# A mixture-of-experts kernel: each expert block's list of places is read into the partitions in another order

## The chip, the cores and the metric

The kernel runs on one core of a Trainium2 chip. The metric is the time of one execution on the device in microseconds (us), as the median of several runs. The engines of the core are called PE (TensorE, matmuls; its weight loads are shown apart as PEld), DVE (VectorE), ACT (ScalarE), POOL (GpSimd) and SP (SyncE, which here only issues transfers). Transfers run on the core's 16 DMA engines, whoever issues them.

## What is computed

One hybrid decoder layer over 16 + 512 tokens of width 1024: a mixer of gated short convolutions and a state-space scan, then a mixture of experts, top 4 of 32, and a final norm. All of it is float32. The change touches only the mixture of experts:

```python
top_vals, top_idx = lax.top_k(logits, TOP_K)              # 4 experts for each of 512 tokens
...
def run_block(args):
    tok, g, e = args
    xb = xt[tok]
    gu = xb @ w_gate_up[e] + b_gate_up[e]
    glu = jnp.minimum(gu[:, :D_FF], SWIGLU_LIMIT)
    lin = jnp.clip(gu[:, D_FF:], -SWIGLU_LIMIT, SWIGLU_LIMIT)
    act = glu * jax.nn.sigmoid(SWIGLU_ALPHA * glu) * (lin + 1.0)
    return (act @ w_down[e] + b_down[e]) * g[:, None]
```

So each expert has 12 MB of weights (1024x2048 and 1024x1024 in float32), which are read once, and gets on average 2048 / 32 = 64 rows of the tokens.

## The kernel before

The mixer runs first (up to about 460 us), then norm, routing and the mixture of experts. What follows is about the last.

**Blocks.** The tokens of an expert take places in a block of `BLOCK` = 96 places, filled from place 0 on; an expert with more than 96 tokens would get more blocks. With these inputs no expert has more than 96, so there are 32 blocks, one for each expert. What is left of a block is unfilled: its entries in `slot_table` hold numbers beyond the range of rows, and the indirect transfers skip them.

**Lanes.** The 1024 columns of a token are cut into `LANES` = 4 quarters of 256 columns (1 KB). Quarter l lives in partitions 32 l to 32 l + 31. A partition holds `GRANULES` = 3 places of the block, 32 x 3 = 96. Which three places stand in which partition is set by how the list is read: `list_rows` reads the 96 entries (token row, output row) once for each lane into `idx_raw`, 32 partitions of 6 integers. Before, partition r of a lane (r = 0 to 31) gets places 3r, 3r + 1, 3r + 2.

**Rows in and out.** For each expert `gather` issues three indirect DMAs (granule n = 0, 1, 2), each of which reads one 1 KB row of `n2_d` (shown as `n_scratch` in the trace) into every partition whose place is filled. `scatter` issues three that write the 1 KB results back into `expert_rows`. Both go through POOL's queue. Around them POOL reads the next list (four DMAs), then waits until lists, rows and results have landed, and passes the lists on through a chain of small copies (`idx_next`, `mid2`, `mid1`, `idx_now`).

**The product.** PE computes a block as 192 products: the 96 rows of the block are the stationary side, in groups of 32 columns, the weights stream past. `TURNS` = "GGGGDDGGDDGGDDDD" weaves the 8 gate-and-up pieces (G) of block j with the 8 half pieces (D) of the down product of block j - 1. DVE turns and bounds what comes out (from L1426 on), ACT does the sigmoid (L927) and copies the down product out (L933, `evict`), which needs `y_room`, POOL's mark that the results before have left.

**The weights.** SP issues the weights as six DMAs of 2 MB for each expert (L498 and L502) into a ring of twelve 1 MB slots. Each waits (L411, `hold`) until PE has used what stood in its slots, and PE waits with `pair_here` until a pair of slots has landed, which is when all 16 DMA engines have delivered their share.

The first two experts don't gather: PE picks their tokens by a product with the 0/1 matrices `chosen` and `chosen1`, made by comparing each token's place with `slot_iota` and `slot_iota1`. Those two hold the numbers of the places in the order in which the block's columns stand, so they have to follow the order of the lists.

Of the kernel before, what the change touches and what calls it, by code (L numbers as in the profile page):

```python
# [33 lines left out]
ds = bass.ds  # L34
# [16 lines left out]
BLOCK = 96  # L51
FIRST, SECOND = 0, 1
BLOCKS_MAX = -(-SEQ // BLOCK)
CAPACITY = BLOCKS_MAX * BLOCK
# [8 lines left out]
LANES, LANE = 4, 32  # L63
GRANULES = BLOCK // LANE
QUARTER = D // LANES
FF_LANE = D // LANES
FF_BLOCKS = FF_LANE // LANE
SLOTS = 6
HALF = LEN // 2
CHALF = (SEQ + 4) // 2  # L70

# [34 lines left out]
def build(nc, xT_d, xrow_d, par_d, wdt_d, win_d, wout_d, rows_d, rw_d, rb_d, moe_d, bgu_d, bd_d, out_d):  # L106
    ctx = ExitStack()
    with ctx:
        def sem(name):
            return ctx.enter_context(nc.semaphore(name))  # L110

        def sb(name, shape, dt=F32):
            return ctx.enter_context(nc.sbuf_tensor(name, shape, dt))
# [4 lines left out]
        table_d = nc.dram_tensor("slot_table", [EXPERTS * CAPACITY + P, 2], I32).ap()  # L118
# [4 lines left out]

        with nc.sbuf_tensor("ring_r", [P, SLOTS * PIECE], F32R) as ring_r:
            pass
        ring = sb("ring", [P, SLOTS * PIECE])
        with nc.sbuf_tensor("late_r", [P, XBC_TILES * LEN], F32R) as late_r:
# [24 lines left out]
        def slot(s):  # L152
            return ring[:, s * PIECE:(s + 1) * PIECE] if s < SLOTS else ring2[:, (s - SLOTS) * PIECE:(s - SLOTS + 1) * PIECE]

        def two_slots(h):
            s = 2 * h
            return ring[:, s * PIECE:(s + 2) * PIECE] if s < SLOTS else ring2[:, (s - SLOTS) * PIECE:(s - SLOTS + 2) * PIECE]

        def one_piece(e, q):
            return moe_d[e, q // 2, :, q % 2 * PIECE:(q % 2 + 1) * PIECE]  # L160
# [3 lines left out]
        def view(region, at, *shape):  # L164
            n = int(np.prod(shape))
            v = region[:, at:at + n]
            if len(shape) == 2:
                v = v.rearrange("p (a b) -> p a b", a=shape[0])
            if len(shape) == 3:
                v = v.rearrange("p (a b c) -> p a b c", a=shape[0], b=shape[1])  # L170
            return v
# [40 lines left out]
        slot_iota = view(late_a, 8192, BLOCK)  # L212
# [3 lines left out]
        slot_iota1 = view(late_a, 8320, BLOCK)  # L216
# [47 lines left out]
        def yk(m, hf):  # L264
# [89 lines left out]
        idx_in, idx_moved, x_in, xT_ready, lane_ready = (  # L354
            sem("idx_in"), sem("idx_moved"), sem("x_in"), sem("xT_ready"), sem("lane_ready"))
# [25 lines left out]
        PART_BANK = [0, 6, 2, 4]  # L381
        HELD = [10, 10, 6, 2, 2, 2] + [0] * (PIECES - SLOTS)
        Z_AT = [(0, 0), (1, 0), (0, 1), (1, 1), (2, 0), (2, 1), (3, 0), (3, 1)]
        Z_USE = [9, 9, 5, 1]

        def pair(k, hf, n):
            return bank[:, 2 * (k % 2) + hf, 0:n]
# [10 lines left out]
        def _(sp):  # L398
# [68 lines left out]
            for m in range(TT):  # L467
                if m == TT - 1:
                    for n in range(4):
                        sp.wait_ge(wout_used, 5 + n)  # L470
                        for q in (2 + n, SLOTS + n):
                            sp.dma_start(slot(q), one_piece(0, q)).then_inc(w_in[q], 16)
# [81 lines left out]
        def _(pool):  # L554
            steps = Steps(pool, pool_steps)
            g = nc.gpsimd
# [9 lines left out]
                            pattern=[[-1, P]], channel_multiplier=1).then_inc(consts, 1)  # L566

            g.affine_select(out=mask[:, :], in_=mask[:, :], compare_op=ALU.is_ge, fill=0.0, base=0,
                            pattern=[[1, P]], channel_multiplier=-1).then_inc(consts, 1)
            g.affine_select(out=lt_bf[:, :], in_=ones_bf[:, :], compare_op=ALU.is_gt, fill=0.0, base=0,  # L570
                            pattern=[[1, P]], channel_multiplier=-1).then_inc(consts, 1)
# [31 lines left out]
            with pool.Fori(1, TT) as i:  # L603
# [1 line left out]
                g.tensor_copy(chunk, xbc[:, :, ds(i * P + META, P)]).then_inc(chunk_ready, 1)  # L605
            pool.wait_ge(chunk_ready, TT)
            pool.wait_ge(tok_done, 2)
            g.iota(slot_iota, pattern=[[1, GRANULES], [GRANULES, LANE]], base=0, channel_multiplier=0,
                   allow_small_or_imprecise_dtypes=True).then_inc(slot_iota_ready, 1)
            g.iota(slot_iota1, pattern=[[1, GRANULES], [GRANULES, LANE]], base=CAPACITY, channel_multiplier=0,  # L610
                   allow_small_or_imprecise_dtypes=True).then_inc(slot_iota_ready, 1)


# [17 lines left out]
            def list_rows(base):  # L631

                for l in range(LANES):
                    pool.dma_start(idx_raw[l * LANE:(l + 1) * LANE, :],  # L634
                                   table_d[ds(base, BLOCK), :].rearrange("(r g) t -> r (g t)", g=GRANULES)).then_inc(idx_in, 16)

            def lane_rows():
                return g.tensor_tensor(idx_next[:, :], idx_raw[:, :], lane_off[:, :], ALU.add)
# [17 lines left out]

            mid1, mid2 = idx_kept
            list_rows(2 * CAPACITY)
            pool.wait_ge(lane_ready, LANES)
            pool.wait_ge(idx_in, 16 * LANES)  # L660
            lane_rows().then_inc(idx_moved, 1)
            pool.wait_ge(idx_moved, 1)
            gather()
            move_rows(mid2, idx_next)
            list_rows(0)
            pool.wait_ge(idx_in, 2 * 16 * LANES)
            g.tensor_tensor(idx_now[:, :], idx_raw[:, :], lane_off[:, :], ALU.add).then_inc(idx_moved, 1)
            pool.wait_ge(idx_moved, 3)
            list_rows(CAPACITY)
            pool.wait_ge(idx_in, 3 * 16 * LANES)  # L670
            g.tensor_tensor(mid1[:, :], idx_raw[:, :], lane_off[:, :], ALU.add).then_inc(idx_moved, 1)
# [14 lines left out]
            with pool.Fori(0, n_blocks - 1) as j:  # L686
# [3 lines left out]
                base = pool.value_load(blocks[0:1, ds(2 * j + 8, 1)], min_val=0, max_val=EXPERTS * CAPACITY)  # L690
# [16 lines left out]
        def _(act):  # L707
# [5 lines left out]
            for c in range(0, KC, 2):  # L713
# [4 lines left out]
            act.sem_inc(free_b, 1)  # L718
            a.activation(t1.rearrange("p (h l) -> p h l", h=2), bank[:, 0:2, 0:HALF], ACT.Sqrt, scale=1.0 / D,
                         bias=eps_col[:, 0:1]).then_inc(rs_root, 1)  # L720
# [15 lines left out]
            def take_tile(i, t):  # L736
                act.wait_ge(tile_done, i * A_TILES + t + 1)
                for hf in range(2):
                    ins = a.copy(stage[:, 3 + hf * HALF:3 + (hf + 1) * HALF], pair(t, hf, HALF))
                    if hf == 0:  # L740
# [780 lines left out]
        def _(pe):  # L1521
# [5 lines left out]
            def mm3(out, n, c, first, width):  # L1527

                for m, (w, x) in enumerate(((w_hi, n_hi), (w_hi, n_lo), (w_lo, n_hi))):
                    ins = mm(out, w[:, n % 2, c * P:(c + 1) * P], x[:, c, first:first + width],  # L1530
                             start=c == 0 and m == 0, stop=c == KC - 1 and m == 2)
                return ins
# [10 lines left out]
            for c in range(KC):  # L1543
# [4 lines left out]
                for hf in range(2):  # L1548
                    ins = mm(bank[:, hf, 0:HALF], ones[:, :], sq8[:, c, hf * HALF:(hf + 1) * HALF],
                             start=c == 0, stop=c == KC - 1)  # L1550
# [4 lines left out]
            def part(t, w, x, c, first, last):  # L1555

                for hf in range(2):
                    ins = mm(pair(t, hf, HALF), w[:, t, c * P:(c + 1) * P], x[:, c, hf * HALF:(hf + 1) * HALF],
                             start=first, stop=last)
# [26 lines left out]
            def a_tile(i, t):  # L1586
                pe.wait_ge(wl_ready, i * A_TILES + t + 1)
                pe.wait_ge(free[t % 2], i * 2 + t // 2 + 1)
                for hf in range(2):
                    for c in range(KC):  # L1590
                        ins = mm3(pair(t, hf, HALF), t, c, hf * HALF, HALF)
                ins.then_inc(tile_done, 1)
# [445 lines left out]
```

## Time and profile before

| | us |
|---|---|
| median of 3 runs | 1506.52 (1505.2 to 1506.59) |
| the profiled execution | 1505.53 |
| its span, first to last instruction | 1503.8 |
| PE busy, matmuls | 1483.7 (99%) |
| of it the experts' products, L1849 | 995.5 |
| POOL busy | 336.4 (22%) |
| TensorE clock granted, mean | 0.999 |

The profiled execution lies 1.0 us under the median. "Busy" of PE is a modelled figure, since matmuls are pipelined, and doesn't tell a PE at its peak from one that is held up a little. An engine's idle time before an instruction is put down to what released it; "issue" is time in which the engine waited for nothing that the profile shows.

### The profile page before, as it was taken

Reading aid. Unit: us, or ns where it says so; the run is one execution under the profiler, and the core shown is the slowest. Engines: PE = TensorE matmul, PEld = TensorE weight load, DVE = VectorE, ACT = ScalarE, POOL = GpSimd, SP = SyncE. Lnnn points to the kernel's source line nnn. Section 1 sums busy time; section 2 is a strip of 40 time slices with the busy share of each in tenths; the row PEclk is TensorE's granted clock in tenths of the full one; section 3 lists DMA queues with packets and bytes.
Section 4 is the critical chain, followed back from the end, with each engine's and each line's share of the span. In section 5 each row is a group of like instructions: output and inputs, shape, how many; then the busy total and the mean of one; then the engine's idle time right before and its main releaser. Section 6 shows DMA issues by size and latency. Waiting matters only on the chain.

```text
span 1503.8 us, 37254 instructions
## 1 busy us (share of the span) xinstructions
PE 1483.7 (99%) x15435; PEld 1069.7 (71%) x15435; DVE 621.5 (41%) x1269; ACT 255.4 (17%) x348; POOL 336.4 (22%) x518
## 2 busy tenths in 40 slices
PE   8999999999999999999999999999999999999998
PEld 6998998977873346777777776777856566567764
DVE  6667988868445322223222232223222232222336
ACT  3533433356231000000000000000000000000002
POOL 1000000000022252223322233222322223222240
PEclk9999999999999999999999999999999999999999
DMA  3642333331438999999999999999999999999977
GB/s 137 245 159 92 113 113 112 131 121 61 164 115 317 400 418 418 416 424 418 419 421 413 425 411 419 415 425 415 422 416 416 413 425 415 416 421 416 424 280 283
DMA packets 53993, 484.31 MB, mean 322 GB/s; under 512 B 14590, under 2 KB 15234, under 8 KB 21570
## 3 DMA queue, kind: packets, MB, share of 16 engines
q1 hardware_dynamic: 38690, 459.13, 74.4%
q0 software_dynamic: 15264, 24.63, 4.4%
q8 instruction: 28, 0.46, 0.1%
q14 instruction: 11, 0.09, 0.0%
HBM read 467.54 MB, written 25.00 MB: 328 GB/s over the span
## 4 chain that ended last, share of the span: by engine, by line
PE 90%; DMA 4%; DVE 4%; issue 1%; ACT 1%; SPq 0%; DVEq 0%; ACTq 0%
PE bank L1849 64%; PE bank L1530 15%; PE bank L1721 6%; DMA n_scratch<-reg_b 1%; DMA ring<-in_moe 1%; DMA ring<-in_w_in 1%; DVE w_lo L983 1%; PE bank L1658 1%; PE bank L1661 1%; PE bank L1673 0%; PE bank L1958 0%; PE bank L1659 0%; PE bank L1688 0%; DVE reg_tq L1073 0%; DMA block_list<-more_i 0%
## 5 line engine op out<-in xcount | busy, mean ns | idle before, releaser
L1849 PE MATMUL bank<-ring,moe_f 128*32 128x512 f32 (+1 forms) x12216 | 995.5, 485 | 4.3 <-DMA ring<-in_moe 2.7
L1849 PEld LDWEIGHTS bank<-ring,moe_f 128*32 128x32 f32 x12216 | 665.6, 110 | 333.2 <-issue 191.5
L1426 DVE STREAM_TRANSPOSE moe_f<-bank 128x768 f32<-128x768 f32 x32 | 31.5, 983 | 700.9 <-PE bank L1849 693.8
L1530 PE MATMUL bank<-n_hi,w_hi 128*128 128x258 f32 (+2 forms) x608 | 190.6, 313 | 3.3 <-DVE w_lo L983 3.3
L1530 PE MATMUL bank<-n_lo,w_hi 128*128 128x258 f32 (+2 forms) x608 | 186.3, 306 | 0.0
L1530 PE MATMUL bank<-n_hi,w_lo 128*128 128x258 f32 (+2 forms) x608 | 186.3, 306 | 0.0
L927 ACT ACTIVATE moe_f<-moe_f 128x768 f32<-128x768 f32 x32 | 27.0, 845 | 830.0 <-DVE moe_f L1432 830.0
L642 POOL DMA_INDIRECT moe_f<-n_scratch,idx_next x96 | 105.7, 1101 | 267.3 <-DVE moe_f L1408 242.4
L1530 PEld LDWEIGHTS bank<-n_hi,w_hi 128*128 128x128 f32 x608 | 114.4, 188 | 11.3 <-issue 3.5
L1530 PEld LDWEIGHTS bank<-n_lo,w_hi 128*128 128x128 f32 x608 | 114.5, 188 | 6.9 <-issue 1.7
L1530 PEld LDWEIGHTS bank<-n_hi,w_lo 128*128 128x128 f32 x608 | 114.4, 188 | 5.5
L649 POOL DMA_INDIRECT expert_rows<-moe_f,idx_now x93 | 95.1, 1022 | 35.4 <-issue 31.7
L655 POOL COPY idx_now<-idx_kept 128x6 int32<-128x6 int32 x31 | 5.8, 187 | 339.3 <-DMA expert_rows<-moe_f,idx_now 339.3
L634 POOL DMA_DIRECT2D idx_raw<-slot_table x140 | 72.4, 536 | 14.1 <-DMA n_scratch<-reg_b 13.5
L619 POOL DMA_INDIRECT slot_table<-val,pos_i x16 | 16.6, 1041 | 196.9 <-DVE pos_i L1326 193.2
L983 DVE TENSOR_TENSOR w_lo<-ring,w_hi 128x1024 fp32r<-128x1024 f32 x48 | 58.4, 1218 | 5.1 <-ACT w_hi L728 5.1
L728 ACT CAST w_hi<-ring 128x1024 fp32r<-128x1024 f32 x48 | 50.4, 1053 | 54.0 <-PE bank L1530 50.5
L1436 DVE TENSOR_SCALAR moe_f<-moe_f 128x96 f32<-128x96 f32 x256 | 51.9, 302 | 0.0
L1432 DVE TENSOR_SCALAR moe_f<-moe_f 128x96 f32<-128x96 f32 x256 | 47.5, 260 | 0.0
L1445 DVE TENSOR_TENSOR moe_f<-moe_f 128x768 f32<-128x768 f32 x32 | 30.7, 958 | 32.3 <-remote 28.2
L1721 PE MATMUL bank<-ring_r 128*128 128x512 f32 x128 | 41.8, 408 | 0.0
L933 ACT COPY moe_f<-bank 128x768 f32<-128x768 f32 x31 | 24.8, 800 | 91.4 <-remote 74.6
(293 smaller groups left out, 1054.1 us busy)
## 6 DMA issues: line engine op xcount, KB each, us to landing
ring<-in_moe SPq DMA_DIRECT2D x184, 2048.0 KB
ring<-in_w_in SPq DMA_DIRECT2D x24, 1024.0 KB, 4.9
ring<-in_moe SPq DMA_DIRECT2D x13, 1024.0 KB, 8.5
expert_rows<-reg_k POOLq DMA_DIRECT2D x8, 1024.0 KB, 6.5
ring<-in_w_out SPq DMA_DIRECT2D x8, 1024.0 KB, 4.8
ring<-expert_rows SPq DMA_DIRECT2D x8, 1024.0 KB, 12.1
ring<-acs_scratch SPq DMA_DIRECT2D x4, 1024.0 KB, 7.0
idx_raw<-slot_table POOLq DMA_DIRECT2D x140, 0.8 KB
```

What stands on the lines that cost most here:

```text
L634: pool.dma_start(idx_raw[l * LANE:(l + 1) * LANE, :], table_d[ds(base, BLOCK), :].rearrange("(r g) t -> r (g t)", g=GRANULES)).then_inc(id ...
L642: g.indirect_dma_start(out=xg[:, n, :], out_offset=None, in_=n2_parts, in_offset=bass.IndirectOffsetOnAxis(ap=idx_next[:, 2 * n:2 * n + 1] ...
L649: g.indirect_dma_start(out=yk_parts, in_=y_sb[:, n, :], in_offset=None, out_offset=bass.IndirectOffsetOnAxis(ap=idx_now[:, 2 * n + 1:2 * n ...
L728: a.copy(w_hi[:, n % 2, :], slot(s)[:, t * KC * P:(t + 1) * KC * P]).then_inc(wh_ready, 1)
L983: v.tensor_tensor(w_lo[:, n % 2, :], slot(s)[:, t * KC * P:(t + 1) * KC * P], w_hi[:, n % 2, :].bitcast(F32), ALU.subtract).then_inc(wl_re ...
L1426: v.transpose(glu.rearrange("p b (g r) -> p g b r", g=GRANULES), gate).then_inc(gate_raw, 1)
L1432: ins = v.tensor_scalar(glu[:, b, :], glu[:, b, :], bias_col(0, b), LIMIT, ALU.add, ALU.min)
L1436: ins = v.tensor_scalar(up[:, b, :], up[:, b, :], bias_col(1, b), 1.0 - LIMIT, ALU.add, ALU.max)
L1445: v.tensor_tensor(act_last if last else act_t, up, sig, ALU.mult).then_inc(act_ready, 1)
L1530: ins = mm(out, w[:, n % 2, c * P:(c + 1) * P], x[:, c, first:first + width], start=c == 0 and m == 0, stop=c == KC - 1 and m == 2)
L1721: ins = mm(bank[:, 2 * m + hf, :], y, w[:, cols], start=t == 0 and n == 0, stop=t == 2 * KC - 1 and n == 2)
L1849: ins = mm(out[l * LANE:(l + 1) * LANE, g * width:(g + 1) * width], x[:, at, g * LANE:(g + 1) * LANE], w[:, l * width:(l + 1) * width], st ...
```

## The change

The list of 96 entries is read into the same 32 partitions of each lane, in the same runs of three entries, but in another order. With `PARTS` = 8, partition r = 4a + b of a lane (a = 0 to 7, b = 0 to 3) now gets places 3(8b + a) to 3(8b + a) + 2. The four partitions 4a to 4a + 3 of a lane so hold one run out of each quarter of the block, where before they held four neighbouring runs. The two `iota` patterns number the columns in the same new order.

```diff
+PARTS = 8
...
-            g.iota(slot_iota, pattern=[[1, GRANULES], [GRANULES, LANE]], base=0, channel_multiplier=0,
+            g.iota(slot_iota, pattern=[[1, GRANULES], [GRANULES, PARTS], [GRANULES * PARTS, LANE // PARTS]], base=0, channel_multiplier=0,
                    allow_small_or_imprecise_dtypes=True).then_inc(slot_iota_ready, 1)
-            g.iota(slot_iota1, pattern=[[1, GRANULES], [GRANULES, LANE]], base=CAPACITY, channel_multiplier=0,
+            g.iota(slot_iota1, pattern=[[1, GRANULES], [GRANULES, PARTS], [GRANULES * PARTS, LANE // PARTS]], base=CAPACITY, channel_multiplier=0,
                    allow_small_or_imprecise_dtypes=True).then_inc(slot_iota_ready, 1)
...
                 for l in range(LANES):
                     pool.dma_start(idx_raw[l * LANE:(l + 1) * LANE, :],
-                                   table_d[ds(base, BLOCK), :].rearrange("(r g) t -> r (g t)", g=GRANULES)).then_inc(idx_in, 16)
+                                   table_d[ds(base, BLOCK), :].rearrange("(b a g) t -> a b (g t)", a=PARTS, g=GRANULES)
+                                   ).then_inc(idx_in, 16)
```

No instruction is added, removed or moved on any engine. POOL's queue in the loop over the experts, from the gather of the next rows to the scatter, stands so before (`moe_f` is the tile of rows in and out, `slot_table` the lists, `expert_rows` the results):

```order
L642 DMA moe_f<-n_scratch,idx_next 128x256 x3
L690 ISA
L690 TENSOR_LOAD blocks
L690 ISA x2
L634 ISA
L634 DMA idx_raw<-slot_table 32x6 x4
L593 REGISTER_ALU
L649 DMA expert_rows<-moe_f,idx_now 8192x256 x3
```

And the same place in POOL's queue after the change (line numbers are one or two higher):

```order
L644 DMA moe_f<-n_scratch,idx_next 128x256 x3
L692 ISA
L692 TENSOR_LOAD blocks
L692 ISA x2
L635 ISA
L635 DMA idx_raw<-slot_table 32x1x6 x4
L594 REGISTER_ALU
L651 DMA expert_rows<-moe_f,idx_now 8192x256 x3
```

Nothing moved; only the pattern of the four list reads has a level more, with the same 6 integers (24 bytes) as its innermost run. Which partitions the three gathers and the three scatters find filled is data, and no row of this kind shows it.

## Rows read from the trace of the kernel before

**Rows 1.** The page: groups of instructions by line (count, busy us, mean ns, idle before)

```profile
L1849 PE MATMUL bank<-ring,moe_f 128*32 128x512 f32 (+1 forms) x12216 | 995.5, 485 | 4.3 <-DMA ring<-in_moe 2.7
```

**Rows 2.** Waits of SP's queue, whole span: us, times, longest us

```profile
SPq L411 <- PE bank L1849: 604.7, 134, 15.7
```

**Rows 3.** Stages: us, engines' busy us (count), clock, DMA share, GB/s

```profile
555.00:1085.00 530.00, 530.00 (x6544) 389.79 (x6540) 129.48 (x360) 27.98 (x34) 157.36 (x239) 1.00 1.01 419
1085.00:1425.00 340.00, 340.00 (x4131) 214.31 (x4127) 77.55 (x213) 17.24 (x21) 99.39 (x152) 1.00 1.00 418
```

**Rows 4.** Waits of the weight loads from 555 to 1085 us, all there are

```profile
engine line waited for: us in total, times, longest us
PEld bank L1849 <- issue: 87.9, 453, 0.6
```

**Rows 5.** Waits of the weight loads from 1085 to 1425 us, all there are

```profile
PEld bank L1849 <- issue: 61.2, 244, 0.6
PEld bank L1849 <- DMA ring<-in_moe: 5.9, 10, 0.8
```

**Rows 6.** Timeline of DVE: L1426, which follows each expert's last G piece

```profile
549.66 0.98 DVE L1426 STREAM_TRANSPOSE moe_f<-bank 128x768 f32<-128x768 f32 x1 [26.00 <-PE bank L1849]
...
580.97 0.98 DVE L1426 STREAM_TRANSPOSE moe_f<-bank 128x768 f32<-128x768 f32 x1 [23.25 <-PE bank L1849]
...
923.56 0.98 DVE L1426 STREAM_TRANSPOSE moe_f<-bank 128x768 f32<-128x768 f32 x1 [22.53 <-PE bank L1849]
...
954.52 0.98 DVE L1426 STREAM_TRANSPOSE moe_f<-bank 128x768 f32<-128x768 f32 x1 [22.76 <-PE bank L1849]
...
1078.89 0.98 DVE L1426 STREAM_TRANSPOSE moe_f<-bank 128x768 f32<-128x768 f32 x1 [22.76 <-PE bank L1849]
```

**Rows 7.** The same, the last expert of the loop

```profile
1424.70 0.98 DVE L1426 STREAM_TRANSPOSE moe_f<-bank 128x768 f32<-128x768 f32 x1 [22.54 <-PE bank L1849]
```

**Rows 8.** DMA from 1085 to 1425 us: packets, MB, share of 16 engines

```profile
DMA packets 13913, 142.01 MB, mean 418 GB/s; under 512 B 4086, under 2 KB 4138, under 8 KB 5614
...
q1 hardware_dynamic: 9337, 135.97, 95.5%
q0 software_dynamic: 4576, 6.04, 4.9%
```

**Rows 9.** Timeline of POOL over one expert

```profile
802.32 1.11 POOL L642 DMA_INDIRECT moe_f<-n_scratch,idx_next  x1 [8.03 <-DVE moe_f L1408]
...
806.25 2.07 POOL L634 DMA_DIRECT2D idx_raw<-slot_table  x4
808.62 1.05 POOL L649 DMA_INDIRECT expert_rows<-moe_f,idx_now  x1 [0.30 <-issue]
...
823.36 0.19 POOL L655 COPY idx_now<-idx_kept 128x6 int32<-128x6 int32 x1 [11.06 <-DMA expert_rows<-moe_f,idx_now]
```

**Rows 10.** Timeline of ACT: the eviction that needs POOL's mark

```profile
837.37 0.80 ACT L933 COPY moe_f<-bank 128x768 f32<-128x768 f32 x1 [2.21 <-remote]
```

**Rows 11.** Waits of the weight loads on weights at the start, 480 to 555 us

```profile
PEld bank L1849 <- DMA ring<-in_moe: 4.5, 2, 2.7
```

## The prediction

> **What bounds the kernel now.** I read the page first. The experts' products hold PE for 995.5 us and PE is said to be idle before them for 4.3 us only [rows 1], so the page alone says "PE". But SP's queue waits for PE to free ring slots in 134 cases [rows 2], while the 16 DMA engines are full: their busy share is 1.01 and 1.00 in both long stretches of the expert loop, at 419 and 418 GB/s [rows 3]. PE and the weight stream are therefore nearly matched, and the question is which of them sets the pace where. The waits of the weight loads answer that. From 555 to 1085 us they never wait for weights [rows 4]. From 1085 to 1425 us they wait for weights 10 times, 5.9 us in all, about once for each of the 11 experts [rows 5]. The marks of DVE's first transpose, one for each expert, give the pace. From 580.97 to 1078.89 there are 16 experts in 497.9 us, 31.12 us each; from 1078.89 to 1424.70 [rows 6, 7] there are 11 in 345.8 us, 31.44 us each. The shortest distance, as from 923.56 to 954.52, is 30.96 us [rows 6]: that is PE undisturbed.
>
> So the reader should see two regimes with the same mean DMA load: first PE alone sets the pace at 31.12 us, and for the last 11 experts the weights come too late, at 31.44 us. A shortage that starts only after 17 experts, with nothing else changed, is a backlog: somewhere a stream needs 31.44 us for an expert that PE asks for every 31.12 us, falls back by 0.32 us each time, and after 16 experts (5.1 us) has used up the time by which weights used to be early. The mean share can't show it, because a pair of slots counts as landed only when the slowest of the 16 engines has delivered. If the mean engine were the slow one, evening out would help nothing; if some engines carry more than the mean, it does.
>
> **What the change moves.** From the reference's inputs I worked out how many places each expert fills: 44 to 85 of 96, 2048 in all. For the eight groups of four partitions in a lane, and with two lanes together (eight partitions), the rows that an indirect gather or scatter of all three granules moves are, as a mean over the 32 experts, before: 24, 24, 24, 23.6, 19, 10, 3.4, 0.1. After: 18.5, 18.0, 17.4, 16.5, 15.3, 14.8, 14.2, 13.4. The sum is the same, 128. I assume that one DMA engine serves one such group in two lanes (32 partitions apart), so that eight of the sixteen have nearly always been full and two empty. Nothing in the rows names engines; what speaks for it is the backlog above, which needs some engines above the mean. The Trainium skill, "DMA: Bandwidth & Descriptors", The descriptor swizzle, gives this very assignment for 128-partition transfers (four neighbouring partitions and the four 32 above them go to one engine); no row here shows it for indirect ones.
>
> *Rows on the busiest engine.* POOL's queue (q0) takes 4.9% of 16 engines over 340 us [rows 8], 16.7 us per engine. At 31.44 us an expert, 340 us are 10.8 experts, so 1.54 us per engine and expert, 24.7 us over all 16. It moves 6.04 MB / 10.8 = 0.56 MB, some 546 rows of 1 KB: 45 ns a row (lists and completion marks are in this, so it is a little high; without them, nearer 40). The busiest engine had 24 in and 24 out, 48 rows, 2.2 us. After, it has 37 rows, 1.7 us. That takes 0.5 us (0.45 at 40 ns) from each expert on the busiest engine.
>
> *What the weights then allow.* The busiest engines need 31.44 us an expert now; less 0.5 that is 30.94 us, under the 31.12 us of PE's own pace, and the backlog doesn't form. Even 0.2 us would do, since the backlog of 5.1 us would then need over 40 experts. So the size of this term doesn't matter, only its sign and that it reaches the slowest engines.
>
> *Gain in the loop.* The last 11 experts go from 31.44 to 31.12 us: 3.5 us. The 5.9 us of waits [rows 5] are an upper bound, as a weight load may wait a little before PE does; PE's own figure of 2.7 us [rows 1] for such waits is a lower one. I take 3.5.
>
> *The start.* The second expert's product waits for weights twice, 4.5 us [rows 11]. That is the time for megabytes of first loads. One gather (third expert, 53 tokens) lies in front of them: on the busiest engine 24 rows become 18, 0.27 us at most. I take 0.1.
>
> *The list reads.* Four a block, 2.07 us of POOL [rows 9]. Their pattern has a level more, which no row here prices. Lower bound nothing; upper bound that each costs double, 2.1 us more of POOL before the scatter. POOL passes its waits at 823.36 us [rows 9] and the eviction that needs its mark starts at 837.37 us [rows 10], so 14 us cover it. The runs stay 24 bytes, so I take nothing. The two `iota` are single instructions well before their use: nothing. PE, DVE and ACT do the same on other columns: nothing.
>
> *More packets.* Eight filled partitions of an engine become five or six, so a packet may hold fewer rows. Lower bound nothing, upper bound one packet more per indirect DMA, six per expert, at the mean of q0, 16.7 x 16 us / 4576 = 58 ns [rows 8]: 0.35 us per expert. Even that leaves 0.15 us of the 0.5 and would merely slow the backlog: 0.17 us an expert instead of 0.32, used up after 30 experts, that is at the end. I take nothing.
>
> Sum against the profiled execution: 1505.5 - 3.5 - 0.1 = 1501.9 us. The median of the runs is 1.0 us above it, so 1502.9 us there, -0.24%.
>
> **Rivals.**
>
> *No change.* The slow stream is not a few engines but all of them: 418 to 419 GB/s in both regimes [rows 3] could be the limit of the whole path, and the busy share leaves no idle time anywhere. Or the filled partitions are dealt to the engines another way, for example every sixteenth partition to the same engine; then the busiest engine has full partitions before as after. Then the backlog grows as now and the time is 1506.5. Against it: the same 418 to 419 GB/s go with 17 experts without one wait; in favour: the share of 1.00 even so, where engines with 46 rows less should show idle time.
>
> *A larger gain.* PE's pace of 31.12 is 0.16 us over its shortest distance of 30.96 [rows 6]. If that too comes from the DMA load (the weight loads' "issue" time [rows 4] hides it), all 28 experts run at 30.96: (1424.70 - 549.66) - 28 x 30.96 = 8.2 us less, 1498.3. Against it: no wait for a DMA is shown there.
>
> *Slower.* The engines of the last group had almost no rows so far. If they are slower at weights by themselves, nothing showed it while they were empty. They kept up with 31.12 us, so their own time is at most that; they now get 13.4 x 2 = 27 rows, 1.2 us. Up to 29.9 us of own time it costs nothing; from 30.2 us on they are slower than the busiest now, and at 31.12 they need 32.3 us, 0.9 us over 31.44, for 30 experts 26 us. A middle case of 30.6 gives 31.8 us, after a backlog of some 8 experts for 20 experts 0.7 us over 31.12, against 3.5 us lost today: some 1517 us. The mean over the engines is 95.5% of 340 us in 10.8 experts, 30.1 us [rows 8], which leaves room for either. The Trainium skill, same page, Latency and other measured facts, says that engines 7 and 15 are usually slower where POOL's queue is used, and by its swizzle those two are exactly this last group. No row here shows engines apart.
>
> *The list reads get costly.* If their 24-byte runs were cut into single integers, 160 more pieces for each of four DMAs fall on 16 engines, 40 each; at the 45 ns of a row 1.8 us an expert, some 50 us in all; it is slower than before from 12 ns each on, when it eats the 0.5 us. The innermost run of 6 integers speaks against it.
>
> **How the numbers follow.** The forecast 0.63, no change 0.21, a larger gain 0.06, slower engines 0.07, costly lists 0.03. About 0.2%, 3.0 us, is what a measurement of this kernel tells from no change, and the forecast of 3.6 us lies just over it: of its 0.63 I put 0.55 at over 3.0 us and 0.08 under. Faster 0.55 + 0.06 = 0.61, within 0.2% 0.21 + 0.08 = 0.29, slower 0.10. The likeliest is 1502.9 us, by itself 1501 to 1504.5 (2 to 5.5 us gained, from the two bounds of the waits). The range takes in no change and its scatter, and part of the larger gain: 1500.5 to 1507; left out are the full larger gain, and both slower cases, 0.16.
>
> **What would show it.** Right: no row "weight loads waiting for ring" between 1085 and 1425 us; the marks of L1426 31.1 us apart up to the last; GB/s in the last stretch a little up; and POOL's wait for the scatter (11.06 us [rows 9]) shorter, since the slowest engine carries less backlog. Wrong: waits for weights that again start in the last third (no change) or earlier (slower); or POOL's list reads well over 2.07 us. The sum fails if the pace without waits is not 31.12 us.

## The result, and the profile after

The change makes the kernel faster by 0.62%: 1496.63 us (median of 6 runs, 1494.67 to 1498.43) against 1506.08 us (6 runs, 1503.85 to 1507.36), ratio 0.9938, 95% interval 0.9926 to 0.9951. The forecast was 1502.9 us, range 1500.5 to 1507: right in direction, but the result lies under the range, and the gain of 9.45 us is more than twice the 3.6 us forecast. The profiled execution took 1494.67 us, its span is 1493.0 us, 10.8 us less than before.

The first thing to look at is what the weight loads wait for in the whole loop over the experts, 545 to 1415 us (columns: us in total, times, longest us):

```profile
engine line waited for: us in total, times, longest us
PEld bank L1851 <- issue: 266.5, 1256, 0.4
```

There is no row for weights any more; before, the last 11 experts had ten such waits [rows 5]. The two stretches of the loop after, in the columns of [rows 3]:

```profile
545.00:1075.00 530.00, 530.00 (x6577) 351.54 (x6570) 129.68 (x359) 27.96 (x34) 161.70 (x242) 1.00 1.01 423
1075.00:1415.00 340.00, 340.00 (x4221) 234.39 (x4215) 82.77 (x232) 18.07 (x22) 104.13 (x154) 1.00 1.01 423
```

The same transfers now run at 423 GB/s from the first expert to the last, so the 418 to 419 GB/s of [rows 3] were not the limit of the path. The DMA share was 1.00 before and is 1.01 now: it doesn't tell an engine that is behind from one that is up to date.

DVE's marks, one for each expert (timeline of DVE after, start us and duration first; answers to [rows 6, 7]):

```profile
546.90 0.98 DVE L1428 STREAM_TRANSPOSE moe_f<-bank 128x768 f32<-128x768 f32 x1 [26.00 <-PE bank L1851]
577.90 0.98 DVE L1428 STREAM_TRANSPOSE moe_f<-bank 128x768 f32<-128x768 f32 x1 [23.34 <-PE bank L1851]
609.31 0.98 DVE L1428 STREAM_TRANSPOSE moe_f<-bank 128x768 f32<-128x768 f32 x1 [22.54 <-PE bank L1851]
...
1074.07 0.98 DVE L1428 STREAM_TRANSPOSE moe_f<-bank 128x768 f32<-128x768 f32 x1 [22.87 <-PE bank L1851]
...
1414.63 0.98 DVE L1428 STREAM_TRANSPOSE moe_f<-bank 128x768 f32<-128x768 f32 x1 [22.81 <-PE bank L1851]
```

The last 11 experts, 1074.07 to 1414.63, take 340.56 us, 30.96 us each. All 28 distances, from 546.90 to 1414.63, make 867.7 us; before they made 1424.70 - 549.66 = 875.0 us [rows 6, 7]. This sum of 28 distances is called "the loop" below. 28 x 30.96 us is 866.9 us, so after, the loop is PE at its undisturbed pace but for 0.9 us. The difference of 10.8 us of the two spans divides into 7.3 us in the loop, 2.8 us ahead of it (549.66 against 546.90) and 0.7 us behind it (79.1 against 78.4 us to the end).

POOL pays for the pattern with a level more. Its timeline over one expert after, against [rows 9]:

```profile
802.62 2.31 POOL L635 DMA_DIRECT2D idx_raw<-slot_table  x4
805.23 1.06 POOL L651 DMA_INDIRECT expert_rows<-moe_f,idx_now  x1 [0.30 <-issue]
...
819.57 0.19 POOL L657 COPY idx_now<-idx_kept 128x6 int32<-128x6 int32 x1 [10.65 <-DMA expert_rows<-moe_f,idx_now]
```

2.31 us for the four list reads instead of 2.07, hidden as foreseen, and 10.65 us of waiting for the scatter instead of 11.06.

### The profile page after: what moved, and what is told of

It is laid out like the page before. It is cut to its first block, busy times and chain, and to the rows that moved or that the text cites. A ratio compares the mean times of both kernels' runs of the same rounds, so it can differ in the third digit from the quotient of the medians.

```text
span 1493.0 us, 37254 instructions
## 1 busy us (share of the span) xinstructions
PE 1476.0 (99%) x15435; PEld 1048.2 (70%) x15435; DVE 621.5 (42%) x1269; ACT 255.5 (17%) x348; POOL 345.3 (23%) x518
## 4 chain that ended last, share of the span: by engine, by line
PE 91%; DVE 4%; DMA 4%; ACT 1%; issue 0%; SPq 0%; DVEq 0%; ACTq 0%
PE bank L1851 64%; PE bank L1532 15%; PE bank L1723 6%; DMA n_scratch<-reg_b 1%; DMA ring<-in_moe 1%; DVE w_lo L985 1%; DMA ring<-in_w_in 1%; PE bank L1660 1%; PE bank L1663 1%; PE bank L1675 0%; PE bank L1960 0%; PE bank L1661 0%; PE bank L1690 0%; DVE reg_tq L1075 0%; DVE reg_tq L1001 0%
## 5 line engine op out<-in xcount | busy, mean ns | idle before, releaser
L1851 PEld LDWEIGHTS bank<-ring,moe_f 128*32 128x32 f32 x12216 | 643.8, 110 | 344.8 <-issue 316.1
L635 POOL DMA_DIRECT2D idx_raw<-slot_table x140 | 80.3, 607 | 13.4 <-DMA n_scratch<-reg_b 12.7
L1001 DVE SCALAR_TENSOR_TENSOR reg_tq<-reg_tq,par 128x528 f32<-128x528 f32 x48 | 36.9, 769 | 5.7 <-DVE reg_tq L997 0.5
```

The costliest lines, as they stand in the source:

```text
L635: pool.dma_start(idx_raw[l * LANE:(l + 1) * LANE, :], table_d[ds(base, BLOCK), :].rearrange("(b a g) t -> a b (g t)", a=PARTS, g=GRANULES) ...
L1001: ins = v.scalar_tensor_tensor(conv_acc[:, 0:LEN], stage[:, k:k + LEN], tap_conv(i * A_TILES + t, k), conv_acc[:, 0:LEN], ALU.mult, ALU.add)
L1851: ins = mm(out[l * LANE:(l + 1) * LANE, g * width:(g + 1) * width], x[:, at, g * LANE:(g + 1) * LANE], w[:, l * width:(l + 1) * width], st ...
```

## The experiments

All times are medians; each ratio is against the kernel before, run between. "Loop" is the sum of the 28 distances in the run's own profile, "waits" are those of weight loads on weights inside it. Four chips were used: e1 to e4 ran on chip 6, e5 to e12 on chip 5, e13 to e16 on chip 12, e17 and e18 on chip 4; for the first two profiles no chip is on record. So differences of a few us between runs of different chips are to be read with care.

| run | what | us | ratio (95%) | loop, us | waits in the loop |
|---|---|---|---|---|---|
| after | the change | 1496.63 | 0.9938 (0.9926 to 0.9951) | 867.7 | none |
| e1 | new order, lists of the loop only | 1496.08 | 0.9930 (0.9914 to 0.9945) | 867.8 | none |
| e2 | new order, first four lists only | 1503.97 | 0.9992 (0.9980 to 1.0003) | 874.6 | yes |
| e3 | PARTS = 4 | 1511.95 | 1.0036 (1.0026 to 1.0046) | 883.7 | yes |
| e5 | before, full gathers | 1505.48 | 0.9995 (0.9984 to 1.0007) | 875.3 | yes |
| e6 | after, full gathers | 1501.37 | 0.9967 (0.9956 to 0.9979) | 871.3 | 3, 1.9 us |
| e7 | PARTS = 16 | 1500.72 | 0.9958 (0.9941 to 0.9974) | 871.6 | none |
| e8 | PARTS = 4, lists read twice | 1524.36 | 1.0115 (1.0098 to 1.0132) | 894.2 | yes |
| e9 | before, no gathered rows | 1498.73 | 0.9952 (0.9936 to 0.9969) | 871.1 | none |
| e10 | before, no scattered rows | 1499.66 | 0.9955 (0.9941 to 0.9969) | 871.8 | none |
| e11 | before, lists read twice | 1511.95 | 1.0052 (1.0032 to 1.0071) | 881.7 | yes |
| e12 | after, lists read twice | 1500.27 | 0.9961 (0.9947 to 0.9975) | 871.7 | none |

### Which lists give the gain: e1 and e2

```diff
             def list_rows(base, spread=False):
...
+                                   (table_d[ds(base, BLOCK), :].rearrange("(b a g) t -> a b (g t)", a=PARTS, g=GRANULES) if spread else
                                     table_d[ds(base, BLOCK), :].rearrange("(r g) t -> r (g t)", g=GRANULES))
...
-                list_rows(base)
+                list_rows(base, True)
```

e1 has this; e2 is the other way round, new order and new `iota` for the first four lists and the old order in the loop.

> The new order only for the lists read inside the loop (experts 4 to 31); the first four lists and the two iota keep the old order. Theory A (the busiest DMA engines are relieved while the loop runs, and both the backlog of the last third and the short stalls of about 0.45 us before it come from them): the loop's marks are 30.96 us apart nearly throughout, about 7 us less than before, and the start stays as before (24.3 us between the first two marks). Rival B (part of the loop's gain was given by the start, whose smaller backlog the loop inherits): the loop gains clearly less than 7 us, 3 to 5 us.

> The new order only for the first four lists (experts 2, 0, 1 and 3) and the two iota; the lists read inside the loop keep the old order. Theory A: the loop is as before (31.1 us, then 31.4 us with waits for weights in the last third), and the total is 0 to 3 us under before, whatever of the 2.2 us at the start belongs to the order. Rival B: the loop starts with less backlog and gains 2 us or more of its own.

e1 gives the whole gain (0.9930) and its loop is 867.8 us; e2 gives nothing that can be told from no change, its loop is 874.6 us. Theory A holds and rival B is out: the start hands nothing on. Waits of the weight loads of e1 over the loop (545 to 1415 us):

```profile
PEld bank L1852 <- issue: 224.5, 1171, 0.5
```

and of e2 over its last experts (1085 to 1425 us):

```profile
PEld bank L1852 <- issue: 106.7, 402, 0.6
PEld bank L1852 <- DMA ring<-in_moe: 7.9, 11, 0.9
```

### The kernel before again: e4 and e16

> The kernel before once more, for a second profile. If the stalls of 0.45 us in the loop and the 4.5 us of waits at the start belong to the kernel, both are there again: a mean of 31.1 us between the marks of experts 3 to 19, 31.4 us and waits for weights after that. If they are chance of one execution, they move or vanish.

> The kernel before a third time. If the ring's backlog is what fixes its loop, the loop takes 875 us again, whatever the number of stalls before the waits for weights begin: with many stalls the waits begin late (after 17 experts), with few early (after 14).

Both profiles moved what had looked like two regimes. In e4 the waits begin earlier than in [rows 4]; its weight loads from 550 to 1085 us:

```profile
PEld bank L1849 <- issue: 131.7, 622, 0.5
PEld bank L1849 <- DMA ring<-in_moe: 2.9, 4, 0.9
```

A "stall" here is a distance some 0.3 to 0.6 us over 30.96 us in which no weight load waits for weights. The first 14 distances of e4 (1505.2 us in all) contain only two, then the pace is 31.47 us in the mean. And yet its loop is 874.9 us, against 875.0 in the first profile, where nearly every third distance of the first 17 had a stall, mostly of 0.45 to 0.5 us, and the waits came after 17 experts. e16 (1505.5 us) had two stalls in 13 distances, waits from then on, one outlier of 33.1 us, and 876.8 us in all; the expectation of 875 was missed by the outlier's 2 us. Stalls on PE's side ahead of the shortage cost nothing before: each only puts the shortage off. This is the point that the forecast missed.

### Mean or fullest engine: e5, e6, e3, e7

e5 and e6 make unfilled places gather row 0 (the rows gathered in excess go nowhere):

```diff
             steps.done(g.memset(pad_tile, PAD * LANES))
+            steps.settled()
+            steps.done(g.memset(pad_tile.rearrange("p (n t) -> p n t", t=2)[:, :, 0:1], 0))
```

> The kernel before, with unfilled places that name row 0 for the gather (not for the scatter), so every gather moves 24 rows on every group of four partitions; the rows gathered in excess are never written out. The fullest groups move as many rows as before (24 in, 24 out), the mean over all rises from 32 to 40 rows an expert. Theory M (the fullest engine sets the pace, at 31.4 to 31.5 us an expert): as before, 1504 to 1508. Rival D (the total over all engines sets it): 8 rows at 45 ns more an expert on the mean, 0.36 us, 10 us in all: 1514 to 1517.

> The same addition in the after-kernel: the gather moves 24 rows on every group, the scatter 13 to 18.5. Fullest 42.5 rows an expert, mean 40. Theory M: the fullest engine needs 31.44 - 5.5 x 0.045 = 31.2 us an expert; 28 x 31.2 less the backlog of about 5 us that the ring absorbs is 868 us for the loop, as after, so 1496 to 1499. Rival D: 0.36 us more an expert than after, about 7 to 10 us: 1504 to 1507.

e5 settles it. It moves a quarter more rows in all and the time doesn't change (0.9995, loop 875.3 us). Its DMA from 1085 to 1425 us, against 418 GB/s and 4.9% for q0 in [rows 8]:

```profile
DMA packets 13896, 143.14 MB, mean 421 GB/s; under 512 B 3804, under 2 KB 3824, under 8 KB 5606
...
q0 software_dynamic: 4570, 7.31, 5.9%
```

The mean engine has more to do, the total rate is higher, and the pace of the last ten experts is 31.46 us, as before (31.47). So the fullest groups set it, and filling the others cost no time here. e6 came out at 1501.37 us, above the 1496 to 1499 expected and below rival D's 1504 to 1507. Its loop is 871.3 us, of which 4.4 us are over 28 x 30.96: five distances with a stall of 0.5 us, and a short wait for weights in each of the last three experts (31.13, 31.52 and 31.49 us):

```profile
PEld bank L1853 <- issue: 155.8, 814, 0.6
PEld bank L1853 <- DMA ring<-in_moe: 1.9, 3, 0.8
```

So a shortage just begins at the end of e6. The missed range is mostly stalls, which come from the chip or the session and not from the kernel (below).

e3 and e7 change one number, `PARTS = 4` and `PARTS = 16`.

> The after-kernel with PARTS = 4: partition 8a + b of a lane holds places 3(4b + a) on. Also a spread, but over groups of eight partitions: every second group of four is full (24 rows for each gather, as before), the others get 6 to 10 rows. Theory A (one engine serves one group of four partitions, and the fullest one sets the pace): eight engines are as full as before, so the time is that of before, within 2 us of 1506. Rival C (any finer interleaving of the places helps, by eight neighbouring partitions or by the addresses in memory): close to the after-kernel, 1497 to 1500.

> The after-kernel with PARTS = 16: the fullest group has 22.2 rows for each gather or scatter (44.4 an expert), then 20.8, 18 and less; list reads have an outermost dimension of 16 instead of 8. Theory M: the fullest engine needs 31.44 - 3.6 x 0.045 = 31.3 us an expert, 28 of them less 5 us are 871 us: 1498 to 1501, between after and before, waits for weights only in the last few experts if at all. If only the number of full engines mattered it would equal after (1496).

e3 was a miss on the slow side: 1511.95 us instead of about 1506. Rival C (any finer interleaving helps) is refuted clearly, and that full groups of four stay the bound agrees; but with as many rows as before it ran slower than before. Its stretches:

```profile
550.00:1085.00 535.00, 533.69 (x6557) 310.24 (x6552) 129.95 (x359) 27.94 (x34) 163.93 (x242) 1.00 1.01 416
1085.00:1425.00 340.00, 337.98 (x4096) 143.16 (x4091) 80.77 (x229) 18.07 (x22) 104.51 (x150) 1.00 1.00 413
```

413 GB/s and 31.81 us an expert over the last ten. e7 hit its number, 1500.7 us, but not by the mechanism expected: its weight loads never wait for weights in the loop.

```profile
PEld bank L1851 <- issue: 150.3, 783, 0.6
```

Its loop of 871.6 us is 866.9 plus stalls alone (nine distances of 31.4 us or more). So, by the dealing assumed, 44.4 rows on the two fullest engines and 41.6 on the next two don't yet make a shortage within 28 experts. This does not fit e6 if the fullest engine alone counts: e6 has 42.5 rows there and runs short. What e6 has more of is the total, 40 rows on the mean against 32. By an estimate from its own trace (12.58 MB of weights and 7.29 MB of q0 in 330 us) it would need 429 GB/s at 30.96 us an expert, and no long stretch of any run here moved more than 423. So with the rows evened out the total may be the next limit, close behind; no run separates the two.

The traces also hold something that shows the skew itself. The semaphore of each weight transfer is raised 16 times, once for each share that has landed. For the transfers between 1085 and 1415 us of which all 16 marks are in the trace, the medians are:

| run | transfers | first to last mark, us | widest gap between two marks |
|---|---|---|---|
| before | 34 | 10.0 | after the 8th, in all 34 |
| e3, PARTS = 4 | 36 | 10.5 | after the 8th, in all 36 |
| e5, before, full gathers | 38 | 9.7 | after the 6th (22) or 8th (16) |
| e7, PARTS = 16 | 38 | 6.3 | after the 14th, in all 38 |
| after | 44 | 4.0 | after the 11th, in all 44 |
| e9, no gathered rows | 43 | 2.1 | none steady |

Before, eight of the 16 shares come first (within 1.6 us) and the other eight 7.2 to 10.0 us after the first one. From 555 to 800 us the whole spread is still 4.6 us there: the backlog grows, as the prediction had inferred. With PARTS = 16 just two shares are late. Eight and two are the numbers of nearly full engines that the assumed dealing gives. After, the eight late ones are gone and the weights are complete 4.0 us after their first share.

### Is PARTS = 4 slower by its list reads: e8, e11 and e12

The list reads have 4 as their outermost source dimension in e3, 8 in the after-kernel, 32 before. Each of these runs reads every list of the loop a second time into a spare tile:

```diff
                 list_rows(base)
+                list_rows(base, idx_spare)
...
-                hold((idx_in, j * (16 * LANES) + 80 * LANES), (x_in, j * (16 * GRANULES) + 32 * GRANULES),
+                hold((idx_in, j * (32 * LANES) + 96 * LANES), (x_in, j * (16 * GRANULES) + 32 * GRANULES),
```

> The kernel with PARTS = 4, which was slower than before (1512), with each list inside the loop read twice (the second time into a spare tile that nobody uses): four small DMAs more an expert, with an outermost source dimension of 4. Theory L (PARTS = 4 loses because its list reads are dealt to few engines and cost those 0.3 us an expert): the cost doubles, another 0.3 us for some 28 experts, 1519 to 1522. Rival E (it loses because its full engines are others than before, two of them neighbours in some shared resource or slower by themselves): the list reads cost next to nothing, 1511 to 1513.

> The kernel before with each list inside the loop read twice (second time into a spare tile). Here the source's outermost dimension is 32, so the four extra small DMAs are dealt to all 16 engines. Theory L (what made PARTS = 4 slow, and twice as slow when doubled, is that its list reads go to 4 engines): spread over 16 they cost next to nothing, 1505 to 1508. Rival (any further small DMA of this kind costs some 0.4 us an expert, however it is dealt): 1516 to 1519.

> The after-kernel with each list inside the loop read twice. Its list reads have an outermost source dimension of 8. Theory L, if the cost grows with what one engine gets: between nothing and a little, and PE's pace still hides it: 1496 to 1499. If 8 engines are already as bad as 4, 0.4 us an expert less the room of the after-kernel: 1500 to 1505.

e8 is 12.4 us over e3 (which ran on another chip; by the two ratios it is 0.8%, 11.9 us) and e11 6.7 us over the kernel before (1511.95 against 1505.26 in the same session). So where weights are short, a list read is not free. Over the last ten experts the pace goes from 31.81 (e3) to 32.2 us (e8), and from 31.47 (before) to 31.73 us (e11): 0.4 and 0.26 us for four DMAs of 768 bytes. (The profiled run of e8 was the slowest of its four, 6.8 us over their median; the medians give 0.44 and 0.24 us.) Theory L was half right: the cost is higher with an outermost dimension of 4 than with 32, but "next to nothing" for the old pattern was wrong. The difference of the two, 12.4 less 6.7 us, is 5.7 us, and e3 lies 6.5 us over the kernel before (1511.95 against 1505.41). So the list reads account for about what e3 loses. Rival E, that its full engines are slower by themselves, is not needed for it, but no run rules out a share of it. The after-kernel hides the list reads, since PE sets its pace: e12 is 3.6 us over the after-kernel, but no weight load waits for weights in its loop, and its 4.8 us over 866.9 are again stalls. The Trainium skill ("DMA: Bandwidth & Descriptors", section "Why a DMA increments its semaphore by 16 and not by 1") says that a DMA runs on the largest number of engines up to 16 that divides the slowest dimension of both sides, with an exception for some direct copies from POOL's queue; by the rule it is 4 engines in e3, 8 in the after-kernel and 16 before. The costs of 4 and 32 are in that order, but no run shows which engines served the lists.

### How much the rows cost at all: e9 and e10

```diff
-                                         bounds_check=SEQ * LANES - 1, oob_is_err=False).then_inc(x_in, 16)
+                                         bounds_check=LANES - 1, oob_is_err=False).then_inc(x_in, 16)
```

e10 does the same to the scatter's bound.

> The kernel before, order untouched, with the bound of the gather lowered so that all rows but those of token 0 are skipped: the experts from the third on compute on stale rows, the scatter is whole. The fullest engines move 24 rows an expert instead of 48. Theory M: they need 31.44 - 24 x 0.045 = 30.4 us an expert, less than PE's 30.96, so no backlog forms and the loop takes 28 x 30.96 = 867 us plus stalls of 0.45 us after the loop's branch, if any: 1494 to 1498. Theory S1 (these stalls come from the gather, which is issued just after the branch): none here, and as many as in the kernel before (about one expert in three) in the run without scatter. Theory S2 (they come with the skew between full and empty engines or the backlog): few or none in either. Theory S3 (they belong to PE's loop alone): in both as before.

> The kernel before, order untouched, with the bound of the scatter lowered so that all rows but those of token 0 are skipped: the experts' results up to the last but one are not written out, the gather is whole. Same load on the fullest engines as without the gather, 24 rows. Theory M: 1494 to 1498 as there. Theory S1: stalls of 0.45 us after about one branch in three; S2: few or none; S3: as before.

With half of the rows gone from the fullest engines there is no shortage: 0.9952 and 0.9955, no wait for weights. That is not better than the after-kernel's 0.9938, which moves all rows, but was measured on another chip than e9 and e10. The times are 1 to 2 us above the range expected, by 8 and 10 stalls. Theories S1 and S2 fall, since the stall is about as frequent with either transfer gone (8 and 10 of 28). The timeline of DVE in e9 shows one, 31.44 us between the first two of these marks and 30.96 us between the next ones:

```profile
702.84 0.98 DVE L1426 STREAM_TRANSPOSE moe_f<-bank 128x768 f32<-128x768 f32 x1 [22.76 <-PE bank L1849]
734.28 0.98 DVE L1426 STREAM_TRANSPOSE moe_f<-bank 128x768 f32<-128x768 f32 x1 [22.51 <-PE bank L1849]
765.24 0.98 DVE L1426 STREAM_TRANSPOSE moe_f<-bank 128x768 f32<-128x768 f32 x1 [22.77 <-PE bank L1849]
```

### Does the order make the stall rare: e13, e14, e15, e17, e18

The after-kernel had 2 such stalls, these others 7 to 10. Five single runs:

> The after-kernel once more, for a second profile. It tells whether the few stalls of 0.45 us after the loop's branch (2 of 28 experts in the first profile, 9 to 11 in runs that have no shortage of weights either) belong to the new order or to that one execution. Order: 2 or 3 again, loop 867.7 us. Chance of the execution: another count, up to 10, loop 868 to 872 us.

> The after-kernel a third time, same question and same numbers: 2 or 3 stalls if they belong to the order, any count from 2 to 10 if not. In either case no weight load waits for weights inside the loop.

> The after-kernel with the bound of the gather lowered so that all rows but those of token 0 are skipped (experts from the third on compute on stale rows). With the old order this had 9 stalls in 28 experts. If the order is what makes them rare: 2 or 3. If it is chance: about any count.

> The after-kernel once more, on the same chip as the next run. Theory G (the stall of 0.45 us behind the loop's branch is frequent or rare by the chip or the session, whatever the kernel: all kernels run together with each other had it rarely, 1 or 2 times before weights ran short, or all had it often, about every third expert): as often as in the next run. Theory O (the order makes it rare): 1 or 2 here, 7 or more in the next run.

> The kernel before with its gather's rows skipped (all but those of token 0), which had 8 such stalls in 28 experts in its first run. Theory G: as many as in the run just before on this chip, 1 or 2 in both or 7 or more in both. Theory O: 7 or more again, against 1 or 2 there.

| run | kernel | us | loop, us | stalls |
|---|---|---|---|---|
| e13 | after | 1494.82 | 867.4 | 1 |
| e14 | after | 1495.91 | 867.4 | 1 |
| e15 | after, no gathered rows | 1496.13 | 867.7 | 2 |
| e17 | after | 1496.10 | 868.1 | 3 |
| e18 | before, no gathered rows | 1496.08 | 867.8 | 2 |

After e13 to e15 it looked like the order. e18 refutes that: the same kernel as e9, with the old order, has 2 stalls where e9 had 8, beside an after-kernel with 3. Counted by session, e1 to e4 had them rarely, e5 to e12 often, e13 to e18 rarely, whatever the kernel (the kernels short of weights counted ahead of their shortage). So the count doesn't come from the change. Both sessions with frequent stalls (e5 to e8, e9 to e12) were on chip 5, and the others on chips 6, 12 and 4, so whether it belongs to the chip or to the session can't be told. Frequent stalls cost a kernel without a shortage 3 to 4 us (loops of 871.1 to 871.8 us in e7, e9, e10 and e12, of 867.4 to 868.1 us in the runs of this table), and the kernel before nothing. The after-kernel itself was never run on chip 5; e12, with its lists read twice, is the nearest, at a ratio of 0.9961. From the ratios of the four kernels without a shortage there (0.9952 to 0.9961), the gain where stalls are frequent is by estimate 0.4 to 0.5% and not 0.62%; that is not measured. The single runs e17 and e18 also say that on one chip the after-kernel is as fast as one that gathers no rows at all.

## Why the prediction was wrong in size

**What bounds the kernel.** The reading was right that the page's "PE" hides a shortage of weights and that the slowest engine, not the mean one, makes it (e5). It was right that there is a backlog, and that the change keeps it from forming (e1; no waits after; the eight late shares in the table of marks, which are gone after).

**The step that failed** is the gain in the loop: "The last 11 experts go from 31.44 to 31.12 us: 3.5 us". It took 31.12 us, the mean distance of the stretch without waits, as PE's own pace. That mean held stalls of PE's own which have nothing to do with the weights, and which were free as long as the fullest engines set the end: e4 had far fewer of them ahead of its shortage and needed 874.9 us all the same. The prediction had named this as its weak point: "The sum fails if the pace without waits is not 31.12 us." The time of a loop that ends in shortage is the fullest engines' work less the room in the ring: 28 x 31.47 - 875.0 = 6.1 us of room. The same difference is 5.5 to 7.8 us in e2, e3, e4, e5, e8 and e11, whose loops range from 874.6 to 894.2 us. What had to be set against it was PE's undisturbed pace, 28 x 30.96 = 866.9 us, plus the stalls of that execution. That gives up to 8.1 us; the two profiles show 7.3 us. The number 31.12 can come true: on chip 5, where stalls are frequent, the four kernels without waits (e7, e9, e10, e12) needed 871.1 to 871.8 us, 31.11 to 31.14 us an expert, and there the term of 3.5 us would have been about right. What failed was to take the stalls of one profile for a property of the kernel. The rival "a larger gain" had this number, 8.2 us and 1498.3 us, but at a chance of 0.06 and with the cause that the DMA load makes the stalls, which e18 doesn't bear out.

**The busiest engine's 0.5 us.** Right in sign; its size was never needed. e7, with only 3.6 rows an expert less on the fullest engines (and fewer of them), already shows no waits.

**The start.** Put at 0.1 us; the profiles differ by 2.8 us up to the third mark. But this part varies by itself: the distance between the first two marks was 24.33, 24.81 and 22.54 us in three profiles of the kernel before, 22.14, 22.36, 21.46 and 21.95 us in four of the after-kernel, and 22.77 and 22.31 us in e1 and e11, whose first lists have the old order. e2 puts all of the first lists' effect at 0.08%, with no change inside its interval. How much of the 1 to 2 us is due to the order stays open.

**The list reads** were put at nothing with POOL's time as the only cost. POOL's time rose by 0.24 us an expert, hidden. That such small DMAs also cost a loop short of weights 0.06 us or more each (e11, e8) was not seen, and with PARTS = 4 it probably decides the sign.

**The rivals.** "No change" is refuted by the result, by e5 and by 423 GB/s after. "Slower" by newly filled engines did not happen; e5, which fills all of them in the gather, shows no loss. The Trainium skill ("DMA: Bandwidth & Descriptors", section "Latency and other measured facts") has engines 7 and 15 as usually slower; no loss of time from that shows here, and no run shows the two apart from the others.

**What is not shown**: which DMA engine serves which partitions. e3 (neighbouring groups of four, one full, one not: no gain), e5 and the numbers of late shares agree with the assignment assumed, but no row names engines. Whether the fullest engine or the total would be the limit after the change is open too (e6 against e7). The cause of the stall of 0.45 us also stays open.

## What to carry to other kernels

When a stream is short only late in a loop, compute the whole loop as the slow engine's work less the room that buffers give, and compare it with the other side's undisturbed pace, not with its mean pace so far: small stalls ahead of a shortage are free before the change and aren't part of the bound. When indirect DMAs skip unfilled places and a full-rate stream shares the DMA engines, look at how the filled places lie: here packing them made eight of 16 shares of each weight transfer late, and spreading them evenly over groups of four partitions (not of eight, e3) cured it. Keep the reads of index lists few, and their outermost dimension wide. A mean DMA share can't show such a skew; the 16 marks of one transfer's semaphore can. Repeat the profile of the kernel before: two regimes in one profile can be one bound and a chance.

## What was not expected of the hardware

Four reads of 768 bytes an expert, in runs of 24 bytes, slow a loop that is short of weights by 0.26 us an expert when their outermost source dimension is 32 (e11) and by 0.4 us when it is 4 (e8). A second point is the stall of about 0.45 us in PE's loop, which on chip 5 hits about every third pass (8 and 10 of 28 in e9 and e10) and on the others nearly none; the profile calls it "issue". The timeline of the kernel before shows it as two gaps between weight loads, where 0.17 us is usual:

```profile
805.87 0.19 PEld L1849 LDWEIGHTS bank<-ring,moe_f 128*32 128x32 f32 x6 [0.43 <-issue]
806.65 0.26 PEld L1849 LDWEIGHTS bank<-ring,moe_f 128*32 128x32 f32 x7 [0.58 <-issue]
```

Last, DMA busy shares of 1.00 and 1.01 stood beside 409 to 423 GB/s (e8 and after): a full share is no measure of how much more could be moved.
